# Rows for experts 0 and 1 by one-hot products on TensorE, and chunks turned five and three

## The reference

```
h = rmsnorm(x)                                   # 512 x 1024
group = argmax(h @ w_group + b)                  # 8 groups
top2  = top_k(h @ w_expert + b of that group)    # 2 of 8 experts: 64 experts in all
for each expert e, with the rows of h that picked it:
    y = (silu(rows @ w_gate[e]) * (rows @ w_up[e])) @ w_down[e]     # 1024 -> 256 -> 1024
x += sum over the two picks of weight * y
```

## Time and profile before

| | us |
|---|---|
| median of 3 runs | 1628.82 (1625.43 to 1629.88) |
| profiled execution | 1631.93 |
| its span, first to last instruction | 1630.2 |
| PE busy | 1437.2 (88%) |
| DVE, ACT, POOL busy | 607.3, 340.9, 248.9 |
| mean DMA rate | 295 GB/s |
| mean granted TensorE clock | 0.99 |

### The profile page before, as it was taken

How to read it: one execution, slowest core, us unless ns; L and a number is a source line. 1 busy time by engine, 2 the same in 40 slices (tenths; PEclk the granted TensorE clock), 3 DMA queues, 4 the chain that set the end, 5 groups by cost and what they waited for, 6 DMA issues and landing times.

```text
span 1630.2 us, 24202 instructions
## 1 busy us (share of the span) xinstructions
PE 1437.2 (88%) x8999; PEld 900.5 (55%) x8999; DVE 607.3 (37%) x1523; ACT 340.9 (21%) x983; POOL 248.9 (15%) x293
## 2 busy tenths in 40 slices
PE   8999999999899988787778999999899977778785
PEld 3655466655566655555555555655566655555453
DVE  2145677742532222212123556423522222222225
ACT  2122377741110000000001345412100000000000
POOL 1122100000211111111112233000211111111112
PEclk9999999999999999999999999999999999999998
DMA  7115140026699999999999401473899999999997
GB/s 294 47 52 209 50 156 1 1 119 236 240 365 430 429 429 429 429 430 430 429 430 421 184 1 78 181 297 116 340 393 426 430 429 428 429 430 430 428 430 297
DMA packets 44661, 480.91 MB, mean 295 GB/s; under 512 B 11262, under 2 KB 11790, under 8 KB 24944
## 3 DMA queue, kind: packets, MB, share of 16 engines
q1 hardware_dynamic: 28144, 450.17, 66.0%
q0 software_dynamic: 15296, 25.61, 4.5%
q10 hardware_dynamic: 1152, 4.19, 0.6%
HBM read 462.37 MB, written 47.19 MB: 313 GB/s over the span
## 4 chain that ended last, share of the span: by engine, by line
PE 57%; DMA 33%; DVE 6%; issue 2%; ACT 1%; another core or an unknown queue 0%; POOL 0%; SPq 0%; DVEq 0%; ACTq 0%; POOLq 0%
DMA sb_arena<-moe_w 32%; PE ps L1187 12%; PE ps L1381 7%; PE ps L1602 7%; PE ps L1196 7%; PE ps L1708 2%; PE ps L1738 2%; PE ps L1723 2%; PE ps L1568 2%; PE ps L1428 2%; PE ps L1456 2%; PE ps L1452 1%; PE ps L1288 1%; PE ps L1509 1%; PE ps L1539 1%
## 5 line engine op out<-in xcount | busy, mean ns | idle before, releaser
L1187 PE MATMUL ps<-sb_arena,sb_x_block 128*64 128x256 f32 x4096 | 473.5, 384 | 89.2 <-DMA sb_arena<-moe_w 88.7
L1187 PEld LDWEIGHTS ps<-sb_arena,sb_x_block 128*64 128x64 f32 x4096 | 419.9, 197 | 196.4 <-issue 133.5
L1196 PE MATMUL ps<-sb_arena,sb_hidden_space 128*64 128x512 f32 x1024 | 247.9, 605 | 46.0 <-ACT sb_hidden_space L918 45.6
L788 POOL DMA_INDIRECT expert_rows<-sb_y_sb,sb_row_now x124 | 133.2, 1074 | 733.0 <-DVE sb_y_sb L1984 665.7
L1983 DVE COPY sb_row_now<-sb_row_of 128x1 uint32 (+1 forms) x124 | 19.1, 154 | 601.3 <-PE ps L1196 586.8
L918 ACT COPY sb_hidden_space<-ps 128x128 f32<-128x128 f32 x128 | 34.1, 267 | 762.6 <-PE ps L1262 757.0
L1196 PEld LDWEIGHTS ps<-sb_arena,sb_hidden_space 128*64 128x64 f32 x1024 | 62.1, 136 | 143.6 <-issue 73.7
L1381 PE MATMUL ps<-sb_sorted_rows,sb_arena 128*128 128x512 f32 x256 | 114.6, 594 | 2.1 <-DVE sb_arena L2226 1.3
L1994 DVE TENSOR_TENSOR sb_x_block<-sb_sorted_rows,sb_moe_gain 128x512 f32<-128x512 f32 x120 | 83.1, 693 | 23.2 <-issue 20.7
L1984 DVE COPY sb_y_sb<-ps 128x512 f32<-128x512 f32 x124 | 84.4, 681 | 0.0
L1381 PEld LDWEIGHTS ps<-sb_sorted_rows,sb_arena 128*128 128x128 f32 x256 | 46.9, 190 | 51.4 <-issue 48.8
(11 more groups left out here) (316 smaller groups left out, 1496.7 us busy)
## 6 DMA issues: line engine op xcount, KB each, us to landing
sb_arena<-moe_w SPq DMA_DIRECT2D x116, 3072.0 KB, 38.0
sb_arena<-moe_w SPq DMA_DIRECT2D x10, 2048.0 KB, 7.7
sb_arena<-moe_w SPq DMA_DIRECT2D x16, 1024.0 KB, 6.2
sb_sorted_rows<-nsa_w_group SPq DMA_DIRECT2D x2, 2048.0 KB, 13.3
sb_arena<-nsa_w_group SPq DMA_DIRECT2D x2, 2048.0 KB, 7.8
sb_sorted_rows<-nsa_w_out SPq DMA_DIRECT2D x1, 4096.0 KB, 12.1
kept_rows<-sb_arena SPq DMA_DIRECT2D x8, 512.0 KB, 4.6
token_rows<-sb_arena ACTq DMA_DIRECT2D x8, 512.0 KB, 2.6
```

The lines of the kernel that those rows point to most:

```text
L788: pool.indirect_dma_start(out=ys_dram.rearrange("r (j n) -> (r j) n", j=2), out_offset=bass.IndirectOffsetOnAxis(ap=row_now[:, u:u + 1], a ...
L1187: last = nc.tensor.matmul(ps[j * BLOCK:(j + 1) * BLOCK, bank, 0:2 * P].rearrange("p (g n) -> p g n", g=2), x_rows[:, :, k], weights[:, 0:2 ...
L1196: last = nc.tensor.matmul(ps[j * BLOCK:(j + 1) * BLOCK, 2, :], hidT[:, c * BLOCK:(c + 1) * BLOCK], weights[:, 2, c * D + j * 512:c * D + ( ...
```

## The change

Experts 0 and 1 no longer have a gather. After each tile's count DVE (`mark_first`) makes `first_hot`: for each token, where it stands among the rows of expert 0 and of expert 1. PE (`select`) multiplies the scaled rows of x in SBUF with it, summed over the four tiles, 32 products of 128x128 by 128; the result lies already turned in two PSUM banks, and `first_blocks` scales it into `x_block`. Half of tile 0's products come before the last tile's count, the rest behind it; `keep_busy(4)` follows them. Of the other `keep_busy` products (3 after the pair product, 1 after the inverse product, 1 before up(0)) none is left. In `route` the first block comes before `token_of` and the second behind it; the block tables' code is now the end of `route`, before the hidden products as before. PE turns five chunks, then does down(1), then three. SP loads slot 5's gate and up once the products are through (they read x there) and issues the 2 MB part of expert 7 + u before the 1 MB part of expert 6 + u.

```diff
 # SP, moe_loads
-                    if t == 1:
-                        sp.wait_ge(first_rows_sent, 32 * (l + 1))
-                        part(RING + 1, RING + 1, 0, 1).then_inc(weights_loaded[RING + 1], 16)
                 sp.wait_ge(last_rows_sent, 32 * (l + 1))
                 sp.wait_ge(logits_done, TILES * (l + 1))
                 part(RING + 2, RING + 2, 1, 3).then_inc(weights_loaded[RING + 2], 16)
-                part(RING + 1, RING + 1, 1, 2).then_inc(weights_loaded[RING + 1], 16)
-                for u in range(PARTED):
-                    sp.wait_ge(up_done, done + u + 1)
-                    part(SLOTS + u, u, 0, 2).then_inc(weights_loaded[u], 16)
-                    sp.wait_ge(down_done, done + u + 1)
-                    part(SLOTS + u, u, 2, 3).then_inc(down_part_loaded[u], 16)
+                sp.wait_ge(selected, l + 1)
+                sp.wait_ge(first_rows_sent, 32 * (l + 1))
+                part(RING + 1, RING + 1, 0, 2).then_inc(weights_loaded[RING + 1], 16)
+                for u in range(PARTED + 1):
+                    if u < PARTED:
+                        sp.wait_ge(up_done, done + u + 1)
+                        part(SLOTS + u, u, 0, 2).then_inc(weights_loaded[u], 16)
+                    if u >= 1:
+                        sp.wait_ge(down_done, done + u)
+                        part(SLOTS + u - 1, u - 1, 2, 3).then_inc(down_part_loaded[u - 1], 16)
 # ACT, moe_act
-                for c in range(CHUNKS):
+                for c in range(5):
                     chunk_half(c)
                 turn_hidden(base + 1)
+                for c in range(5, CHUNKS):
+                    chunk_half(c)
 # PE, count_tile
+                if t >= 1:
+                    pe.wait_ge(hots_ready, l * (TILES + 1) + t)
+                if t >= 2:
+                    pe.wait_ge(picks_summed, l * 2 + t - 1)
+                if t >= 1:
+                    nc.tensor.matmul(ranks_at(t), ones[:, :], picks_until(t), start=True, stop=False)
                 pe.wait_ge(picks_ready, l * TILES + t + 1)
...
+                nc.tensor.matmul(ranks_at(t), below[:, :], pick[:, 2, t, :], start=(t == 0), stop=True).then_inc(counted, 1)
+                if t == TILES - 1:
+                    nc.tensor.matmul(totals, ones[:, :], picks_until(t), start=True, stop=False)
+                    nc.tensor.matmul(totals, ones[:, :], pick[:, 2, t, :], start=False, stop=True).then_inc(counted, 1)
+            def select(l, t, ks):
+                pe.wait_ge(h_ready, l * TILES + t + 1)
+                pe.wait_ge(hots_ready, l * (TILES + 1) + t + 1)
+                for k in ks:
+                    last = nc.tensor.matmul(ps[:, SELECT_BANK + k // 4, k % 4 * P:(k % 4 + 1) * P],
+                                            x_of[l][:, t, :].rearrange("p (m k) -> p k m", k=KD)[:, k, :],
+                                            first_hot[:, t, :, :].rearrange("p e n -> p (e n)"), start=(t == 0 and k % 4 == 0), stop=(t == TILES - 1 and k % 4 == 3))
+                return last
 # PE, end of project_out
+                select(layer, 0, range(KD // 2))
+                count_tile(layer, TILES - 1)
+                select(layer, 0, range(KD // 2, KD))
+                for t in range(1, TILES):
+                    last = select(layer, t, range(KD))
+                last.then_inc(selected, 1)
                 keep_busy(4)
-                count_tile(layer, TILES - 1)
...
-                last.then_inc(inverted, 1)
-                keep_busy(3)
 # PE, moe_pe
-                pe.wait_ge(rows_landed[LAST_CHUNK], 48 * l + 16)
-                turn_rows(LAST_CHUNK, 0)
-                keep_busy(1)
                 up(0, 0, 0)
                 up(1, 1, 0)
                 down(0, 0)
-                for c in range(CHUNKS):
+                for c in range(5):
                     turn_chunk(c)
                 down(1, 1)
+                for c in range(5, CHUNKS):
+                    turn_chunk(c)
 # DVE
+            def mark_first(l, t):
+                dve.wait_ge(counted, l * (TILES + 1) + t + 1)
+                step(v.tensor_scalar(first_rank[:, t, :], pick[:, 2, t, 0:2], -APART, APART, ALU.mult, ALU.add))
+                step(v.tensor_tensor(first_rank[:, t, :], first_rank[:, t, :], ranks_at(t)[:, 0:2], ALU.add))
+                v.tensor_tensor(first_hot[:, t], expert_no[:, 0:BLOCK].unsqueeze(1).to_broadcast([P, 2, BLOCK]),
+                                first_rank[:, t, :].unsqueeze(2).to_broadcast([P, 2, BLOCK]), ALU.is_equal).then_inc(hots_ready, 1)
+            def first_blocks(l, u):
+                rows = ps[:, SELECT_BANK:SELECT_BANK + 2, :].rearrange("p c n -> p (c n)").rearrange(
+                    "p (k e b a) -> p e b a k", k=KD, e=2, b=DEAL)
+                nc.vector.tensor_tensor(x_block[:, u].rearrange("p (a b) k -> p b a k", b=DEAL), rows[:, u],
+                                        moe_gain[:, l, :].unsqueeze(1).unsqueeze(1).to_broadcast([P, DEAL, BLOCK // DEAL, KD]),
+                                        ALU.mult).then_inc(block_ready, 1)
 # DVE, route (tile t - 2 is marked in add_output's loop, tile 3 here)
+                mark_first(l, TILES - 1)
...
+                dve.wait_ge(moe_gain_loaded, 32)
+                dve.wait_ge(selected, l + 1)
+                first_blocks(l, 0)
+                dve.wait_ge(inverted, l + 1)
+                v.tensor_copy(token_of[:, :], ps[:, INVERSE_BANK, 0:CHUNKS]).then_inc(token_ready, 1)
                 step(v.tensor_copy(total, totals))
+                first_blocks(l, 1)
```

More of the change, by code:

```diff
@@ L496, in squared @@
             return n // 2 * (3 * TILES - 1) + t + 1
-        def landed(c, turn):
-            return 16 * turn if c < LAST_CHUNK else 16 * (turn + (turn + 1) // 2)
         def kept_bank(t):
@@ L512, in mla_score_bank, with ranks_at, picks_until @@
             return 4 + 2 * (s % 2)
+        def ranks_at(t):
+            return ps[:, 6, t * EXPERTS:(t + 1) * EXPERTS]
+        def picks_until(t):
+            return pick[:, 2, 0, :] if t == 1 else pick_sum[:, t - 2, :]
         def unit_bank(u):
@@ L626, in mla_loads @@
                 for c in range(CHUNKS):
-                    sp.wait_ge(rows_landed[c], landed(c, 2))
+                    sp.wait_ge(rows_landed[c], 32)
                 sp.dma_start(w_uq, a["mla_w_uq"].rearrange("(c p) n -> p c n", p=P)).then_inc(mla_up_loaded, 16)
@@ L1226, in count_tile @@
             def count_tile(l, t):
-                pe.wait_ge(picks_ready, l * TILES + t + 1)
-                nc.tensor.matmul(ps[:, 6, t * EXPERTS:(t + 1) * EXPERTS], below[:, :], pick[:, 2, t, :],
-                                 start=(t == 0), stop=(t == 0))
-                later = TILES - t
-                last = nc.tensor.matmul(ps[:, 6, (t + 1) * EXPERTS:(TILES + 1) * EXPERTS].rearrange("p (t e) -> p t e", t=later),
-                                        ones[:, :], pick[:, 2, t:t + 1, :].to_broadcast([P, later, EXPERTS]),
-                                        start=(t == 0), stop=(t == TILES - 1))
-                last.then_inc(counted, 1)
+                if t >= 1:
[4 more added lines that the diff above has]
+                    nc.tensor.matmul(ranks_at(t), ones[:, :], picks_until(t), start=True, stop=False)
+                pe.wait_ge(picks_ready, l * TILES + t + 1)
+                nc.tensor.matmul(ranks_at(t), below[:, :], pick[:, 2, t, :], start=(t == 0), stop=True).then_inc(counted, 1)
[10 more added lines that the diff above has]
+                return last
             def keep_busy(n):
@@ L1275, in turn_chunk @@
                 def turn_chunk(c):
-                    pe.wait_ge(rows_landed[c], landed(c, 2 * l + 1))
+                    pe.wait_ge(rows_landed[c], 32 * l + 16)
                     if c == 0:
@@ L1401, in project_out @@
                 logits(layer, turn, TILES - 1, 1)
-                keep_busy(4)
-                count_tile(layer, TILES - 1)
-                pe.wait_ge(hots_ready, 2 * layer + 1)
-                for t in range(TILES):
-                    for e in range(2):
-                        last = nc.tensor.matmul(ps[e * BLOCK:(e + 1) * BLOCK, 0, BLOCK:BLOCK + 1], pair_hot[:, t, e, :],
-                                                pair_tokens[:, t, e:e + 1], start=(t == 0), stop=(t == TILES - 1))
-                last.then_inc(inverted, 1)
-                keep_busy(3)
+                select(layer, 0, range(KD // 2))
[4 more added lines that the diff above has]
+                last.then_inc(selected, 1)
+                keep_busy(4)
             mixers = [0]
@@ L1872, in route @@
                 step.mark(v.tensor_copy(start_i[0:1, l, 0:EXPERTS], start[0:1, :]))
-                dve.wait_ge(inverted, 2 * l + 2)
-                v.tensor_copy(token_of[:, :], ps[:, 0, 0:CHUNKS]).then_inc(token_ready, 1)
-            def block_tables(l):
-                v = nc.vector
-                total, upto, start, blocks, b_upto, b_from = (count[:, i] for i in range(6))
```

(2 more changed lines are left out.)

70 lines of the change are left out of this document (24 added, 46 removed).

## The result

The changed kernel takes 1672.91 us (median of 6 runs, 1669.61 to 1674.32), the kernel before in the same job 1627.26 (6 runs). The ratio is 1.0275 [1.0263, 1.0287]: 45 us slower, where 12 were forecast, and outside the range of 1625 to 1654. The spans are 1672.0 and 1630.2 us.

A forecast was written before the change was run, and what follows sets the result against it. The weight stream was taken as the bound, expert 4's down product setting each stage's end. Stage 0: 5.8 + 1.0 - 0.35 = 6.5; stage 1: 4.6 + 1.0 - 0.35 = 5.3; 11.8 us on 1628.82 gives 1640.6, range 1625 to 1654.

The forecast's parts named there:

- Picking the rows on PE: Selection after the last pick: 56 records at 0.113 us each take 6.3 us, bounds 5.9 to 7.5, ending at 434.3.
- What stands in front of expert 0: Between selection and up(0): four keep_busy products (3.65 us) and the inversion (0.35); up(0) starts at 438.05, 2.7 us won.
- token_of and the tables on DVE: DVE behind the selection: token_of 4.4 us later, tables from 440.0; PE waits 2.5 us for DVE before expert 0's down product.
- Chunk gathers: Gathers issued 4.4 us later meet weight loads; PE waits for chunk 4, up(2) 5.8 us late in stage 0, 4.6 in stage 1.
- the fifth: Share of 430 GB/s given to the gathers while weights flow: 4 KB gather packets beside 16 KB load packets.
- Five and three: Down(1) ahead of chunks 5 to 7 leaves DVE's block 2 uncovered: PE waits 2.6 us before up(2).
- Clock: After PE's waits, part of down(1) and the chunks run at 1.2 GHz: 1.0 us a stage, bounds 0 and 2.5.
- The rival with the clock before the picks: PE idles before the last pick ends and selects at 1.2 GHz: 7 us on top, 1648; chance 0.17.
- DMA order, gain and loss 0: SP's new load order: after up(2), 7 MB have 18 us and need 17.1, so they fit and nothing is lost.
- Expert 4's down product sets the end, one for one: Slot 4's reload after it is where the weight stream last runs dry; whatever moves it moves the stage's end equally.
- one of the signs of being wrong: Wrong if up(2) isn't later against the last pick, or the stage's end moves by another amount than expert 4's down product.
- The faster rival: Up(1) ends 3.3 us earlier in stage 0, 5.1 in stage 1, and that reaches expert 4: 9.1 us won, 1619.7; chance 0.12.

The follow-up runs named there:

- Experiment 1: Changed kernel with the features laid out in contiguous runs, so the selecting products and chunk turns read rows without a stride: 1651.97 us, 1.0144.
- experiment 5: Kernel before, with only down(1) and ACT's turn of its hidden rows moved to after chunk 4 instead of chunk 7: 1639.27 us, 1.0059.
- experiment 7: Changed kernel with SP's weight parts for each stage's last experts back in the order of the kernel before: 1656.40 us, 1.0177.
- experiment 15: Kernel before, with only both first parts of slot 5 (2 MB) held until token_of is written: 1645.67 us, 1.0106.
- experiment 10: Changed kernel with contiguous features, loads of slot 5 and experts 7 on held until all chunks landed, eight chunks before down(1), no keep_busy(4): 1635.21 us, 1.0039.
- Experiment 17: Changed kernel: contiguous features, eight chunks before down(1), no keep_busy(4), SP's old part order, loads from expert 7 on held until chunk 5 landed: 1624.66 us, 0.9985.
- 13: Changed kernel with contiguous feature order, SP's old part order and no keep_busy(4); five and three stay: 1652.28 us, 1.0143.
- 14: Changed kernel with contiguous feature order, SP's old part order and all eight chunks before down(1); keep_busy(4) stays: 1651.59 us, 1.0144.
- experiment 16: Changed kernel: contiguous features, eight chunks before down(1), no keep_busy(4), SP's old part order, loads from expert 7 on held until all chunks landed: 1628.79 us, 1.0009.
- experiment 11: Changed kernel with contiguous features, SP's old part order, all eight chunks before down(1) and no keep_busy(4), no load held: 1646.93 us, 1.0100.
- experiment 2: Kernel before, with only the contiguous feature order (weights, gain and chunk turns), no selection on PE: 1627.27 us, 0.9992.
- experiment 9: Changed kernel with contiguous feature order and SP's old part order; five and three and keep_busy(4) stay: 1640.38 us, 1.0066.
- 3: Changed kernel with SP's loads of slot 5 and of experts 7 on held until all eight chunks have landed: 1658.77 us, 1.0182.
- 4: Changed kernel without the four keep_busy products behind the selection: 1663.78 us, 1.0205.
- 6: Changed kernel with all eight chunks turned before down(1), as in the kernel before: 1664.30 us, 1.0222.
- 12: Changed kernel: contiguous features, SP's old part order, eight chunks before down(1), no keep_busy(4), ACT's share exponentials and table load ahead of the selection wait: 1644.68 us, 1.0096.
- 8: Kernel before, with only the new order of the weight parts on SP's queue: 1628.76 us, 0.9998.

## Why the prediction was wrong

The direction was right, and so was the order of what comes late; the size was off by a factor of almost four. Four terms failed: the selection (6.3 us taken, 13.4 measured), the clock (1.0 taken, 4.6 measured in stage 0), SP's loads (0 taken; slot 5's load waits for the selection, 8 us without a transfer, and the next parts go beside the gathers), and the step that made expert 4's down product the end of the stage.

- *Picking the rows on PE* is the step that failed first: 6.3 us with bounds of 5.9 to 7.5. It is 13.4 us. I took the price of contiguous stationary rows for strided ones, wrote that no row had the strided case, and still drew bounds of a microsecond around the contiguous price. Experiment 1, which takes this back, is 21 us faster (with late signals beside it).
- *What stands in front of expert 0*: keep_busy took 3.44 us and the inversion was as forecast. Up(0) came 17.9 us after the last pick (11.0 forecast), nearly all of it the selection's 7.1.
- *token_of and the tables on DVE*: right. PE waited 2.0 us for DVE's hidden product, forecast 2.5, only 6 us later.
- *Chunk gathers*: the mechanism was right, and so was the fifth: in 451 to 463 the gathers moved 0.98 MB and the weights 3.78. The queues of the changed kernel in 462 to 464 (q1 the loads, q0 the gathers; packets, MB, share), about as many packets of each:

```profile
q1 hardware_dynamic: 47, 0.57, 66.3%
q0 software_dynamic: 55, 0.21, 25.5%
```

  The Trainium skill, DMA: Bandwidth & Descriptors (Queues, rings and completion order), lets one ring drain a lump before the other; these counts, taken over all engines, neither show such lumps nor rule them out. Chunk 4 was turned 24.8 us after the first gather, forecast 19.9 (458.5 after 438.6). What I left out is slot 5's 2 MB, issued at 441.4, just ahead of the gathers: 0.43 MB of weights still moved in 447 to 451, and the gathers had 0.89 MB through by 451, not 1.3. I had also misread: before, the gathers did not have the engines alone from the start (the load queue moved 0.88 MB in 434 to 438), and alone they moved 0.34 MB per us (3.44 in 438 to 448), not 0.42.
- *Five and three*: the uncovered block 2 cost 2.6 us, as forecast. Alone the order costs 10 us (experiment 5), not twice 2.7; the clock behind the wait makes up most of the rest (1.9 us in stage 0).
- *Clock*: 1.0 us a stage with bounds up to 2.5. Down(1) lost 1.7 us and the up products of experts 2 and 3 lost 2.9, together 4.6. I counted the stretch under the wait, not the work behind it. The rival with the clock before the picks did happen for part of the stretch (0.50 in 430 to 432), but the selection's cadence did not change, 10 records in 2 us at 0.50 (430 to 432) as at 1.00 (434 to 436).
- *DMA order, gain and loss 0*: wrong twice. I placed the parts behind up(2), where they fit. The cost arises before it: at 452.1, beside the gathers (experiment 7). And I did not see that slot 5's load now waits for the selection. That is the 8 us of DMA share 0.00 from 434 to 442, and such a wait alone costs 17 us (experiment 15).
- *Expert 4's down product sets the end, one for one*: refuted by experiment 10. In the changed kernel it moved 22.3 us and the end 24.5, which is one of the signs of being wrong that the prediction named. I had read correctly that the weights are the bound of the body, then followed PE to the point where they start anew. The right question was how many megabytes the queue is behind when it last runs dry.
- The faster rival had the gathers and block 2 hidden. Experiment 17 made the gathers hidden and got 3 us, not 9, though up(2) came 4.3 us earlier (457.83 against 462.18). I read this as the rule above: an earlier up(2) only helps as far as it frees slots for loads.

The parts do not add up: mended alone, layout, part order, keep_busy and eight chunks give 21, 16.5, 9 and 8.6 us, 55 of 45, and in all four the late signals are mixed in; three at a time without these give 21 (experiments 13 and 14). So the loss as a whole is explained, since experiment 16 takes all of it back, and its split among the parts is not. They feed one loop. A late gather meets more weights, which make it later; up(2) waits, the slots stay full, the queue runs dry and PE's clock falls.

## What to carry to other kernels

Where a stage is bound by its weight stream, price a change by the megabytes the load queue is behind when it becomes busy for good, and list each load that the change makes wait, also through a buffer that something new still reads. A short gather on which the consumer of the weights depends belongs ahead of the bulk loads: holding the loads behind it gained 18 to 22 us here (experiment 11 against 16 and 17) and 23 between experiments 14 and 16, neither of which has late signals; holding also the load that fills an idle queue gave 6 back (experiment 10, in part perhaps the late signals). Before pricing a product by its shape, look at which operand is stationary and how its elements lie.

## What was not expected of the hardware

- Products with a 128x128 float32 stationary operand whose elements lie 32 bytes apart take 0.239 us per record, with a contiguous one 0.113. The strided price is the same at either clock (10 records in 2 us); the contiguous one is not (experiment 1: 11 records in 429 to 431 at 0.50, 20 in 431 to 433 at 1.00). The chunk turns pay for the stride as well, 18.1 us in place of 13.0 for 288 records (experiment 2).
- After waits of 2.6 to 5.4 us the low clock stayed into the work behind: the changed kernel's granted clock is 0.50 in 464 to 476 and 0.72 in 481.5 to 491.5, with 9.86 us for 64 up records where 7.01 is the full price, and 3.68 for 8 down records where 1.94 is. The length of the wait alone doesn't decide it: behind 2.6 us for block 2 the same 64 records took 8.88 us in experiment 5 and 7.19 in stage 0 of experiment 9.
- In nine of the kernels (experiments 1, 3, 4, 6, 7 and 9 to 12) two signals of PE, the end of up(0) and of the turned hidden block, reached other engines 1 to 3 us after the end of their records (in experiment 9 SP and ACT both went on at 444.5, the records end near 441.8). The chain calls this an unknown queue. In the changed kernel, in the kernel before and its variants (2, 5, 8, 15) and in experiments 13, 14, 16 and 17 it did not occur. It fits the times of experiments 9, 13 and 14, since a later signal to SP leaves the gathers alone for longer, and some of what separates 16 from 10 and 11 may be its absence. Its cause was not found and it was not varied by itself: that stays open.
